# Last state-space group of a two-block kernel: a semaphore for each kind of decay row, another order on VectorE, index products half a tile later, and squares in the one-pass format

## The reference, cut to what matters

```python
# index: 16 heads of 64, in 8 tiles of 128 columns
q_idx = _rope_partial(q_idx.reshape(bsz, seq, 16, 64), pos)
logits = relu(einsum('bqhd,bsd->bqhs', q_idx, k_idx))
score = einsum('bqhs,bqh->bqs', logits, w_idx)        # then top 128 of each row
# state-space mixer, four groups of four heads
lmat = exp(where(tril, seg, -inf))                    # seg: differences of the decay row a_cum
cb = einsum('bclgn,bcsgn->bclsg', cm, bm)
y_diag = einsum('bclsg,bclsgr,bcsgrp->bclgrp', cb, lmat, xdt)
y_off = einsum('bclgn,bcgrpn,bclgr->bclgrp', cm, prev, exp(a_cum))
y = y_diag + y_off + d_skip * xs
g = y * silu(z)
g = g * rsqrt(mean(square(g), axis=-1) + RMS_EPS)     # over the 256 channels of a group
```

## Time and profile before

| | |
|---|---|
| median of three runs | 1727.95 us (1725.14 to 1729.54) |
| the profiled execution | 1727.94 us, of it 1726.2 us from the first to the last instruction |
| TensorE matmul busy | 1710.0 us, 99% |
| VectorE, ScalarE, GpSimd busy | 42%, 36%, 40% |
| granted TensorE clock, mean | 0.997 |

### The profile page before, as it was taken

The page is one execution under the profiler, slowest core; times in us unless marked ns, Lnnn a source line. Parts: engine busy times, 40 slices in busy tenths (PEclk is TensorE's granted clock), DMA queues, the critical chain, the costliest instruction groups (busy, mean ns, idle before and its releaser), DMA issues.

```text
span 1726.2 us, 21738 instructions
## 1 busy us (share of the span) xinstructions
PE 1710.0 (99%) x7958; PEld 1399.2 (81%) x7958; DVE 723.7 (42%) x1246; ACT 615.8 (36%) x851; POOL 697.6 (40%) x301
## 2 busy tenths in 40 slices
PE   9999999999999999999999999999999999999997
PEld 8888888888888888888888888887668787788886
DVE  4323321222111135211752744738679634465226
ACT  6434433443222224212642323423452434362120
POOL 4433343333444444445244434334226333325451
PEclk9999999999999999999999999999999999999999
DMA  6433323323233332543154342434123222227332
GB/s 225 121 92 92 90 87 92 99 88 94 92 98 97 98 90 94 170 122 106 65 197 129 116 132 88 134 103 118 49 76 98 84 75 73 83 61 269 121 97 98
DMA packets 56222, 186.16 MB, mean 108 GB/s; under 512 B 5928, under 2 KB 6184, under 8 KB 55376
## 3 DMA queue, kind: packets, MB, share of 16 engines
q1 hardware_dynamic: 46512, 160.19, 30.2%
q10 hardware_dynamic: 9632, 24.88, 4.1%
HBM read 176.57 MB, written 8.47 MB: 107 GB/s over the span
## 4 chain that ended last, share of the span: by engine, by line
PE 94%; DVE 3%; issue 1%; ACT 1%; POOL 0%; DMA 0%; SPq 0%; DVEq 0%; ACTq 0%; POOLq 0%
PE bank L456 92%; PE bank L460 2%; POOL w_lo L409 0%; DVE feats L1309 0%; DVE padded L1587 0%; DMA probsT<-decay_dram 0%; ACT w_hi L870 0%; DVE probs L1588 0%; DVE probs L1589 0%; DVE padded L1586 0%; DVE planes_lo L1529 0%; DVE kT L1688 0%; DVE wide L1697 0%; DVE bank L1522 0%; DVE tmp L1413 0%
## 5 line engine op out<-in xcount | busy, mean ns | idle before, releaser
L409 POOL TENSOR_TENSOR w_lo<-raw,w_hi 128x1024 fp32r<-128x1024 f32 x272 | 663.0, 2439 | 987.3 <-ACT w_hi L870 987.2
L456 PE MATMUL bank<-planes_hi,w_hi 128*128 128x512 f32 (+1 forms) x1792 | 705.8, 394 | 0.9 <-DVE planes_lo L1529 0.4
L456 PE MATMUL bank<-planes_lo,w_hi 128*128 128x512 f32 (+1 forms) x1792 | 691.8, 386 | 0.0
L456 PE MATMUL bank<-planes_hi,w_lo 128*128 128x512 f32 (+1 forms) x1776 | 686.4, 387 | 0.0
L870 ACT ACTIVATE w_hi<-raw 128x1024 fp32r<-128x1024 f32 x276 | 292.7, 1060 | 940.8 <-PE bank L456 909.3
L456 PEld LDWEIGHTS bank<-planes_hi,w_hi 128*128 128x128 f32 x1792 | 337.0, 188 | 84.1 <-issue 17.1
L456 PEld LDWEIGHTS bank<-planes_lo,w_hi 128*128 128x128 f32 x1792 | 337.3, 188 | 68.6 <-issue 3.3
L456 PEld LDWEIGHTS bank<-planes_hi,w_lo 128*128 128x128 f32 x1776 | 334.0, 188 | 67.8
L456 PE MATMUL bank<-w_hi,planes_hi 128*128 128x512 f32 x480 | 188.1, 392 | 0.0
L456 PE MATMUL bank<-w_hi,planes_lo 128*128 128x512 f32 x480 | 187.0, 390 | 0.0
L456 PE MATMUL bank<-w_lo,planes_hi 128*128 128x512 f32 x480 | 186.9, 389 | 0.0
(11 more groups left out here) (283 smaller groups left out, 1329.9 us busy)
## 6 DMA issues: line engine op xcount, KB each, us to landing
raw<-in_stream SPq DMA_DIRECT2D x281, 512.0 KB, 3.6
h_rows<-feats ACTq DMA_DIRECT2D x4, 1024.0 KB, 9.1
feats<-in_x_t SPq DMA_DIRECT2D x7, 512.0 KB, 9.3
out<-feats ACTq DMA_DIRECT2D x7, 512.0 KB, 2.7
rope_q<-cum_dram ACTq DMA_DIRECT2D x8, 256.0 KB, 3.0
bias<-in_x_rows ACTq DMA_DIRECT2D x2, 1024.0 KB, 6.1
probs<-in_x_rows ACTq DMA_DIRECT2D x2, 1024.0 KB, 7.9
rope_q<-decay_dram SPq DMA_DIRECT2D x8, 256.0 KB, 5.4
```

The costliest lines, as they stand in the source:

```text
L409: nc.gpsimd.tensor_sub(w_lo[:, s, :], raw[:, s, :], w_hi[:, s, :].bitcast(fp32)).then_inc(lo_ready, 1)
L456: return nc.tensor.matmul(o, a, b, start=start, stop=stop)
```

## The change

1. `decay_loaded` becomes two lists, one for LB and one for EB. `segments` waits for its LB row alone; `operands` waits also for its EB row.
2. In the last turn VectorE does the rotations of tiles 24 and 25 behind `operands`, with those of 26 and 27. ScalarE does the four exponentials of the decay rows (`ssd_exps`) in front of the take of tile 24, where it did them behind that of tile 25. TensorE does `ssd_states(3)` in front of tile 25, where it did it behind.
3. The index products move by half a tile: tile 28 held products of index tiles 0 and 1, tile 29 those of 2 and 3, tile 30 those of 4. Now tile 28 holds 0, tile 29 holds 1 and 2, tile 30 holds 3 and 4. ScalarE's ReLUs move with them. VectorE's order of sums, of `ssd_gated(3)` and of the rotations of tiles 28 to 31 stays.
4. In all four groups the squares are cut in two one-pass parts: VectorE adds a copy to `sq_hi` and a subtraction to `sq_lo` at the end of `ssd_gated`, and TensorE does two one-pass products where it did one in float32. The ones are copied once to that format behind the first block.

```diff
-        decay_kept, decay_loaded = sem("decay_kept"), [sem(f"decay_loaded{r}") for r in range(4)]
+        decay_kept, decay_loaded = sem("decay_kept"), [[sem(f"decay_loaded{of}{r}") for r in range(4)] for of in range(2)]
...
-                after = {6 * GROUPS + 4: idx_between(0, 1), 6 * GROUPS + 5: idx_between(2, 3)}.get(n, {})
+                after = {6 * GROUPS + 4: idx_between(None, 0), 6 * GROUPS + 5: idx_between(1, 2)}.get(n, {})
...
-                mm(M[:, :], ones[:, :], SQ[0]).then_inc(ssd_mm, 1)
+                mm(M[:, :], ones_r[:, :], sq_hi[:, :], True, False)
+                mm(M[:, :], ones_r[:, :], sq_lo[:, :], False, True).then_inc(ssd_mm, 1)
...
+                if it == GROUPS:
+                    ssd_states(g)
                 ssd_tile(6 * it + 1)
                 if g < 0:
                     prepare()
-                else:
+                elif it < GROUPS:
                     ssd_states(g)
...
-            project(tile_at(T_IDX, 6), T_IDX + 6 - SK - 1, after=idx_between(None, 4))
+            project(tile_at(T_IDX, 6), T_IDX + 6 - SK - 1, after=idx_between(3, 4))
...
-                    idx_tile((m, p), 2 * k - 8, 2 * k - 7)
+                    idx_tile((m, p), None if k == 4 else 1, 2 * k - 8)
...
+                if k == 0 and it == GROUPS:
+                    for r in range(4):
+                        ssd_exps(it - 1, r)
...
-                dve.wait_ge(decay_loaded[r], 32 * (g + 1))
+                dve.wait_ge(decay_loaded[0][r], 16 * (g + 1))
...
                 dve.wait_ge(ssd_exp, EXP_STEPS * g + r + 1)
+                dve.wait_ge(decay_loaded[1][r], 16 * (g + 1))
...
-                signal(V.tensor_add(SQ[0], SQ[0], SQ[1]), ssd_vec, VEC_STEPS * g + 13)
+                step(V.tensor_add(SQ[0], SQ[0], SQ[1]))
+                step(V.tensor_copy(sq_hi[:, :], SQ[0]))
+                signal(V.tensor_sub(sq_lo[:, :], SQ[0], sq_hi[:, :].bitcast(fp32)), ssd_vec, VEC_STEPS * g + 13)
...
-                if it == GROUPS:
-                    conv_tile(6 * it)
-                conv_tile(6 * it + 1)
+                if it < GROUPS:
+                    conv_tile(6 * it + 1)
                 ssd_carry(g)
...
                 if it == GROUPS:
-                    conv_tile(6 * it + 2)
-                    conv_tile(6 * it + 3)
+                    for k in range(4):
+                        conv_tile(6 * it + k)
```

More of the change, by code:

```diff
@@ L148, in block_kernel @@
         gate = sb("gate", [P, S])
+        tmp_at = nc.sbuf_base
         tmp = sb("tmp", [P, S])
@@ L152, in block_kernel @@
         probs = sb("probs", [P, QB, S])
+        probsT_at = nc.sbuf_base
         probsT_at = nc.sbuf_base
@@ L160, in block_kernel @@
         ones = sb("ones", [P, P])
+        ones_r = sb("ones_r", [P, P], fp32r)
+        sq_hi = nc.alloc_sbuf_tensor_at("sq_hi", [P, S], fp32r, offset=probsT_at + 2 * 4 * S)
+        sq_lo = nc.alloc_sbuf_tensor_at("sq_lo", [P, S], fp32r, offset=tmp_at)
         par = sb("par", [P, NPAR])
@@ L351, in load_decay @@
                     row = SSD_HEADS * of + 4 * g + r
-                    sp.dma_start(bufs[r], decay_dram[row:row + 1, :].to_broadcast([P, S])).then_inc(decay_loaded[r], 16)
+                    sp.dma_start(bufs[r], decay_dram[row:row + 1, :].to_broadcast([P, S])).then_inc(decay_loaded[of][r], 16)
             m0, p0 = tile_at(T_SSD, 6)
@@ L1243, in _ @@
                         act.dma_start(rope_i, rope_idx).then_inc(rope_i_loaded, 16)
-                    if it and k == (2 if it < GROUPS else 1):
+                    if 0 < it < GROUPS and k == 2:
                         for r in range(4):
@@ L1247, in _ @@
             t = tile_at(T_IDX, 6)
-            idx_tile(t, None, 4)
+            idx_tile(t, 3, 4)
             take(t, QI[6], T_IDX - SK + 7)
@@ L1578, in _ @@
             back_and_norm(0, T_BACK1)
+            step(V.tensor_copy(ones_r[:, :], ones[:, :]))
             SK = BACK_TILES
```

## The result

| | median | runs | range |
|---|---|---|---|
| before | 1728.07 us | 12 | 1725.14 to 1729.61 |
| changed | 1731.12 us | 12 | 1728.98 to 1732.30 |

A forecast was written before the change was run, and what follows sets the result against it. TensorE, busy 99% of the span, was taken to bound the kernel. 1727.94 - 4.7 (old wait and clock) - 1.6 (squares) + 5.9 (new waits) + 1.7 (clock) = 1729.2 us; overall range 1721.5 to 1733.5, the forecast's own 1727 to 1733.

The forecast's parts named there:

- The old wait: TensorE's 3.0 us stand near 1208 for a ScalarE ReLU; its removal, with 1.7 us of clock, was to save 4.7 us.
- Squares: Two one-pass products per group on TensorE in place of one float32 product, sparing 1.6 us over four groups.
- First wait: In tile 29 TensorE was to wait 1.7 us for a ReLU before product (2, 3).
- S: Start of product (tile 1, i = 3), from which the times of the wait in tile 29 were counted.
- Second wait: After tile 30 TensorE was to wait 1.6 us at the squares of group 3, 0.35 without copy and subtraction.
- T: Start of product (3, 3), at place 7 of tile 30, from which later times were counted.
- Third wait: In tile 31 TensorE was to wait 2.6 us before product (5, 1) for the rotation of tile 29.
- Nothing new waits: Rival: the half tile is enough for VectorE, no new TensorE waits, 1721.6 us; chance 0.13.
- VectorE gets in front of GpSimd: Rival: VectorE's operations start before the low parts, waits shrink to about 0.3, 0.3 and 1.2 us, 1723.5 us; chance 0.10.
- The clock stays low through all three: Rival: low clock after each new wait and one stretch longer, loss over 6.8 us, above 1732.6 to 1735; chance 0.15.
- Clock: One fall of TensorE to 1.2 GHz, behind the wait in tile 31, costing 1.7 us; bounds none and three.
- the rotation of tile 31: Behind tile 31 no cost was counted; a low part in its way could cost up to 2.4 us, less its room.

The follow-up runs named there:

- e3: The kernel before with only separate semaphores for the two decay rows: 1723.53 us, ratio 0.9977.
- e8: The kernel before with only the new order of rotations, exponentials and states: 1723.71 us, ratio 0.9974.
- e2: The kernel before with only the index products moved half a tile later: 1730.55 us, ratio 1.0020.
- e9: The kernel before with separate decay-row semaphores and one-pass squares, old order and old product places: 1721.58 us, ratio 0.9964.
- e5: The changed kernel with the squares back in float32, without the copy and subtraction: 1730.11 us, ratio 1.0015.
- e1: The changed kernel with the index products put back to their old places: 1721.69 us, ratio 0.9969.
- e6: The changed kernel with ScalarE's first rounding in tiles 29 to 31 behind both index tiles' ReLUs, so low parts come later: 1733.32 us, ratio 1.0029.
- e11: The kernel before, unchanged, profiled once more to see the clock a second time: 1729.23 us.
- e7: The changed kernel with the rotation of tile 28 before sum_scores(1) and that of tile 29 before sum_scores(3): 1727.99 us, ratio 0.9999.
- e4: The kernel before with only the squares in one-pass format: 1727.32 us, ratio 0.9995.

## Why the prediction was right

The median is 1731.12 us; 1729.2 was forecast, with 1727 to 1733 as the forecast's own range. The mechanism is the one forecast, in each place. What is off is the size of one term, the clock.

- **The old wait.** Gone, with `segments(3)` right behind the mask. e3 gives -4.5 us for the semaphores where I had -4.7. The result leaves that term standing, but my reason for part 2, "costs nothing that I can find", was half the truth: e8 shows that it takes 4.3 us by itself, nearly the same. The takings of parts 1, 2 and 3 (2.7 of the 3.0 in e2) don't add. In the kernel before VectorE was late by about what any one of them gives, and beyond that the take of tile 27 is the bound.
- **Squares.** Two products 0.23 us apart, as forecast. 1.95 us spared by the medians against my 1.6; by the timelines 1.7 to 1.8 are the squares' own, about 0.44 a group (e9). What the profiled executions differ by beyond that lies ahead of the first squares, where the starts scatter. The copy took 0.43 us, where I took 0.49 and allowed 0.69: the row of the scalar operation inside SBUF was the nearer one, as chosen.
- **First wait.** 1.74 us, forecast 1.7: (2, 3) stood at S + 9.80, forecast S + 9.6 or a little later, due at S + 7.98.
- **Second wait.** 1.48, forecast 1.6; the squares at T + 11.47, forecast T + 11.5. In e2 and e5, without copy and subtraction, 0.3, forecast 0.35.
- **Third wait.** 2.45, forecast 2.6; (5, 1) at T + 16.03, forecast T + 16.0. GpSimd did end last, so that e5's 1.2 us less on VectorE shortened the sum of second and third wait only from 3.9 to 3.0.
- **The rivals.** "Nothing new waits" (1721.6) is what e1 and e9 do, and the changed kernel doesn't. "VectorE gets in front of GpSimd" did not happen: all three operations stood behind the low part and took 2.10, 2.28 and 2.10 us. e6 shows 1.4 us of the first wait to be that, as put there (1.7 to 0.3), and also that moving the low parts away is no cure. The Trainium skill (SBUF — State Buffer, Who interferes with whom) has the port as an exclusive lock that the one issued first holds; the traces agree, with ends 0.55 us behind GpSimd's. "The clock stays low through all three" did not happen either: two falls in one profile, one in the other. Its figures don't fit each other either: three falls are 5.1 us and give 1732.6, and a loss of over 6.8 would be above 1734.3.
- **Clock: the mis-sized term.** I counted one fall, 1.7 us, behind the third wait. That fall came in both profiles (1.7 and 1.6). A second one, behind the first wait of 1.74 us, came in one of them, so that the term was 3.4 there. With the term at 3.4 my sum is 1730.9 us, and the median is 1731.12. How often each fall comes in the twelve runs can't be read, since only two were profiled; that their median lies a fall above the forecast, and their range over 3.3 us, agrees with a second fall in many of them, and is not shown by it. Five of the twelve took 1732.01 to 1732.30 us, 0.7 to 1.0 more than the profiled one with its two falls. A fall of double length, as in e2 and e11, would do that; it is not shown for them.

**What the half tile cost is shown from both sides:** taken out of the changed kernel it gives 9.4 us (e1), put alone into the kernel before it costs 2.5 (e2). The two differ by 6.9 us, of which some 4.5 are the old wait and its clock, most of which it takes away in the kernel before. Of the other 2.4, 0.6 are waits (5.0 us in all in e2, 5.7 in the changed kernel); the rest would be the clock, and that stays open. e6 and e7 tried to keep it and pay less. Both removed the waits that they aimed at, and both found another for the rotation of tile 31, in tile 32, which I had called possible and priced at nothing. Whether some other order keeps the half tile without a wait was not tried, and there is nothing to win by it: with parts 1 and 4 alone no wait is left in the stage.

## What to carry to other kernels

When several edits aim at one wait, run each alone: here any of three took most or all of its 3.0 us, and the one that cost something later was not needed. A place in the bottleneck engine's order is worth as much as its distance from the place before: moving two dependent products out of different tiles into the same one took the time between them that another engine had been using. Lay such a chain out from one known start with each operation's duration and each stretch on a shared port; it gave three waits to 0.2 us here, and when a cure moves the port's other user, lay out the next place that it meets too.

## What the runs showed of the hardware that was not expected

- TensorE's clock doesn't answer to the same wait in the same way twice. Behind a wait of 3.0 us it kept 2.4 GHz in e4, and fell to 1.2 GHz in two profiles of the kernel before, for 1.6 and 2.7 us of loss. By windows of 0.5 us even the moment differs: 1.3 us after TensorE had gone on in one (at 1211.4, the product at 1210.09), 1.0 us before it in the other (1209.2, the product at 1210.27). Behind one of 1.7 us it fell in one profile and not in the next.
- The scatter of a kernel goes with it. The kernels with no wait of TensorE in this stage range over 0.4 to 0.9 us (e1, e3, e8, e9), those with waits over 1.6 to 4.7 us.
- A VectorE operation with two SBUF inputs that met a low part of GpSimd ended 0.55 us after it in the places read here, less than the 0.69 that it takes alone. `SCALAR_TENSOR_TENSOR` with SBUF inputs is held as well: 2.75 and 2.93 us for 0.75 in e7.
- GpSimd is held too, when VectorE was first. In e7 a low part that takes 2.39 us alone took 2.70, where an operation of VectorE had begun 0.29 us before it (in the kernel before, one at 1195.47 took 2.86, with VectorE's begun at 1195.39):

```profile
1264.23 2.70 POOL L414 TENSOR_TENSOR w_lo<-raw,w_hi 128x1024 fp32r<-128x1024 f32 x1 [8.96 <-ACT w_hi L878]
```

```profile
1263.94 0.75 DVE L1320 SCALAR_TENSOR_TENSOR bias<-gate,widxN,bias 128x512 f32<-128x512 f32 x1
```
